# Gate and up projections as 2x2 block products with seven products, in a two-block transformer kernel

## The reference

```python
# first block, D_FF = 2816
h = rmsnorm(x, norm_ffn)
x = x + (silu(h @ w_gate) * (h @ w_up)) @ w_down
...
# second block, D_FF_2 = 4096
h = _rmsnorm(x, mlp_norm_w)
x = x + square(relu(h @ w_up)) @ w_down
```

## Time and profile before

| what | value |
|---|---|
| median of 3 runs | 3381.11 us (3380.43 to 3384.27) |
| the profiled execution | 3385.8 us, its span 3384.0 us |
| TensorE busy | 3128.2 us, 92% |
| VectorE, ScalarE, GpSimd busy | 36%, 31%, 30% |
| moved by DMA | 177.27 MB, 52 GB/s on average |

### The profile page before, as it was taken

How to read it: one execution, slowest core, us unless ns; L and a number is a source line. 1 busy time by engine, 2 the same in 40 slices (tenths; PEclk the granted TensorE clock), 3 DMA queues, 4 the chain that set the end, 5 groups by cost and what they waited for, 6 DMA issues and landing times.

```text
span 3384.0 us, 36901 instructions
## 1 busy us (share of the span) xinstructions
PE 3128.2 (92%) x14350; PEld 2388.2 (71%) x14350; DVE 1232.6 (36%) x2192; ACT 1065.8 (31%) x1490; POOL 1015.0 (30%) x424
## 2 busy tenths in 40 slices
PE   5989888888989999999999898896999999999998
PEld 3556556566678788888887665564777788888887
DVE  4347777766132111111113555554553211112122
ACT  3235554444433211111113344443553211111110
POOL 4322233221234343243246200013102332323241
PEclk8879999899999999999999999997999999999999
DMA  5311112111152111111111311001002111111112
GB/s 158 98 31 32 38 32 57 38 39 49 51 168 84 48 48 51 44 50 50 44 48 43 107 30 31 14 24 31 19 4 81 44 54 46 50 43 56 44 50 68
DMA packets 261934, 177.27 MB, mean 52 GB/s; under 512 B 20724, under 2 KB 248948, under 8 KB 261236
## 3 DMA queue, kind: packets, MB, share of 16 engines
q1 hardware_dynamic: 261816, 175.69, 18.0%
HBM read 142.60 MB, written 25.20 MB: 50 GB/s over the span
## 4 chain that ended last, share of the span: by engine, by line
PE 79%; DVE 8%; ACT 5%; issue 5%; POOL 2%; DMA 1%; SPq 0%; ACTq 0%; DVEq 0%; POOLq 0%
PE big L832 64%; PE big L990 4%; PE tbank L1013 3%; PE obank L1031 3%; PE big L964 2%; PE obank L1028 2%; PE big L861 1%; DVE tally_a L1665 1%; DVE dprob L1729 1%; POOL w_lo L1909 1%; DVE prob L1729 1%; ACT prob L1218 1%; DVE g_lo L1775 0%; DMA x_res<-x_spill 0%; ACT mpt L1176 0%
## 5 line engine op out<-in xcount | busy, mean ns | idle before, releaser
L832 PE MATMUL big<-g_hi,w_hi 128*128 128x512 f32 x3328 | 1074.4, 404 | 61.5 <-ACT gst_b L1250 21.1
L832 PE MATMUL big<-g_lo,w_hi 128*128 128x512 f32 x3328 | 1040.6, 394 | 0.0
L832 PE MATMUL big<-g_hi,w_lo 128*128 128x512 f32 x3328 | 1037.1, 393 | 0.0
L832 PEld LDWEIGHTS big<-g_hi,w_hi 128*128 128x128 f32 x3328 | 609.0, 191 | 265.7 <-issue 142.9
L832 PEld LDWEIGHTS big<-g_lo,w_hi 128*128 128x128 f32 x3328 | 633.0, 190 | 137.0 <-issue 0.7
L832 PEld LDWEIGHTS big<-g_hi,w_lo 128*128 128x128 f32 x3328 | 631.5, 190 | 137.4 <-issue 0.4
L1909 POOL TENSOR_TENSOR w_lo<-w_raw,w_hi 128x1024 fp32r<-128x1024 f32 x99 | 241.4, 2439 | 593.0 <-ACT w_hi L1152 593.0
L1998 POOL TENSOR_TENSOR w_lo<-w_raw,w_hi 128x1024 fp32r<-128x1024 f32 x76 | 181.9, 2393 | 64.2 <-ACT w_hi L1371 64.2
L1840 DVE TENSOR_TENSOR x_res<-big,x_res 128x1024 f32 x40 | 49.0, 1225 | 382.1 <-PE big L832 382.1
L2024 POOL TENSOR_TENSOR w_lo<-w_raw,w_hi 128x1024 fp32r<-128x1024 f32 x40 | 95.7, 2393 | 273.2 <-ACT w_hi L1399 273.2
L1176 ACT ACTIVATE pt<-tbank 128x512 f32<-128x512 f32 (+1 forms) x160 | 88.2, 555 | 221.3 <-PE tbank L1013 221.3
(11 more groups left out here) (268 smaller groups left out, 3498.0 us busy)
## 6 DMA issues: line engine op xcount, KB each, us to landing
w_raw<-in_w_up SPq DMA_DIRECT2D x54, 512.0 KB, 3.9
w_raw<-in_w_in SPq DMA_DIRECT2D x51, 512.0 KB, 4.2
w_raw<-in_w_down SPq DMA_DIRECT2D x48, 512.0 KB, 3.9
w_raw<-in_w_gate SPq DMA_DIRECT2D x22, 512.0 KB, 3.8
rot<-rope_in SPq DMA_DIRECT2D x68, 128.0 KB, 2.3
g_spill<-gst_b SPq DMA_DIRECT2D x16, 512.0 KB, 3.0
x_res<-x_spill SPq DMA_DIRECT2D x2, 4096.0 KB, 14.0
w_raw<-in_w_out SPq DMA_DIRECT2D x16, 512.0 KB, 4.3
```

The lines of the kernel that those rows point to most:

```text
L832: ins = pe.matmul(out[0:m, HALF * h:HALF * h + HALF], w[slot][:, col:col + m], x[:, HALF * h:HALF * h + HALF], start=(n == 0 and q == 0), ...
```

## The change

Both feed-forward blocks are changed in how the up side is computed. A job takes two column tiles together: gate and up tile of the same features in `mlp1` (22 jobs), two neighbouring up tiles in `mlp2` (16 jobs). The job is a 2x2 block product: the weights are A (tile 1 or 2, chunks 0 to 3 or 4 to 7), the activations B (chunks 0 to 3 or 4 to 7, tokens 0 to 511 or 512 to 1023). It is done by seven block products in place of eight, of sums and differences of blocks:

- Weight operands per job: A11, A12 and A22 as they are, and the sums S1 = A21 + A22, S2 = S1 - A11, S4 = S2 - A12, S3 = A21 - A11, in 128x512 each. GpSimd makes the four sums and all seven low parts, ScalarE the seven high parts. The order of use is A11, S1, A12, S4, S2, A22, S3. Each operand has one place, which is free again when the job before has done that product. Both raw tiles are loaded together, once the S3 low part of the job before is done.
- Activation operands, once per block: B11, B21, B22 and T1 to T4, each 4 chunks of 128x512 in a high and a low part. VectorE makes them during `out` and right behind it, in place of `g2h` and `g2l`; T4 and T3 and their low parts, and that of T2, come last.
- A product is 4 x 3 matmuls of 128x512 into a PSUM bank of its own: `tbank` (2), `obank` (2) and three halves of `big`. ScalarE copies out the first two, and VectorE adds the others in seven steps into two rows (`crow`, two buffers), which are the tile pair. VectorE scales both rows by `r_rep` and forms the activation: SiLU between by ScalarE in `mlp1`, a square of the positive part for each row in `mlp2`.
- The activations go to DRAM (`a_spill`, 512 KB per tile) and come back ahead of the down side, in groups of (8, 4, 4, 6) tiles in `mlp1` and 4 of 8 in `mlp2`. ScalarE makes the high part of a reloaded tile, VectorE the low part (`act_lo`). All up jobs come first, then all down groups. The down products stay as they were, 6 matmuls per chunk.
- The first matmul of the sum of squares now stands behind the first product of the first job. The last group of `mlp1` keeps its norm work.

```diff
+    B11, T1, B21, B22, T2, T4, T3 = range(7)
+    A11, S1, A12, S4, S2, A22, S3 = range(7)
...
+    READ_AT = {2: 1, 4: 2, 3: 3, 6: 5, 5: 7}
...
+    BLOCKED = ["mlp1", "mlp2"]
+    groups1 = [(0, 8), (8, 4), (12, 4), (16, 6)] if "mlp1" in BLOCKED else [(0, 8), (8, 8), (16, 6)]
...
+    def down_buffers(stage, gi):
+        return (g1h, g1l) if gi % 2 == (1 if stage in BLOCKED else 0) else (g2h, g2l)
...
+    def slot_free(stage, q, n):
+        if n:
+            return s_st.sem, s_st.base(stage) + 7 * (n - 1) + q + 1
+        w = last_outs(stage)
+        return s_big.at("w", w[0]) if q < 2 else (s_big.at("w", w[1]) if q < 4 else s_big.at("ss", "ffn" if stage == "mlp1" else "mlp2"))
...
+                banks = [tbank[0][:, :], tbank[1][:, :], obank[0][:, :], obank[1][:, :], big[p0][:, 0:HALF], big[p0][:, HALF:T], big[1 - p0][:, 0:HALF]]
+                def block_product(q, at_job):
+                    pe.wait_ge(s_al.sem, at_job(7, al0 + q + 1))
+                    for k in range(4):
+                        for z, (w, x) in enumerate(((ah, bh), (ah, bl), (al, bh))):
+                            ins = pe.matmul(banks[q], w[q][:, P * k:P * k + P], x[q][:, k, :], start=(k == 0 and z == 0),
+                                            stop=(k == 3 and z == 2))
+                    ins.then_inc(s_st.sem, 1)
...
+                with pe.Fori(1, NJ, 1) as i:
+                    for q in range(7):
+                        if q < 2:
+                            pe.wait_ge(s_ar.sem, i * 2 + (ar0 + q - 1))
+                        else:
+                            pe.wait_ge(s_dr.sem, i * 7 + (dr0 - 7 + READ_AT[q]))
+                        block_product(q, lambda m, c: i * m + c)
...
+                            if gi == 0:
+                                pe.wait_ge(s_dr.sem, dr0 + 7 * NJ)
+                                pe.wait_ge(s_ar.sem, ar0 + 2 * NJ)
+                            ready = (lambda k: s_xlo.at(stage, f0 + k)) if u == 0 else (lambda k: None)
...
+        def weight_hi(stage, q, n):
+            ah, _, az = a_ops[last_outs(stage)[1] % 2]
+            src = block_source(q, *w_raw)
+            if q in (A11, A12, A22):
+                for t in range(2):
+                    act.wait_ge(*s_ur[t].at(stage, n))
+            else:
+                act.wait_ge(*s_as.at(stage, q, n))
+            act.wait_ge(*slot_free(stage, q, n))
+            act.activation(ah[q][:, :], az[q][:, :] if src is None else src, ACT.Copy).then_inc(*s_ah.mark(stage, q, n))
...
+                for m in range(NJ):
+                    c = crow[m % 2]
+                    ahead = m + 1 < NJ
...
+                    read(m, 0, c[1][:, 0:HALF])
+                    read(m, 1, c[1][:, HALF:T], -1.0)
+                    if m == 0:
+                        act.wait_ge(*s_bf.at(out_stage, T4))
...
+                        weight_hi(stage, S3, 0)
+                    if ahead:
+                        for q in (A11, S1, A12):
+                            weight_hi(stage, q, m + 1)
...
+                    if ahead:
+                        for q in (S4, S2):
+                            weight_hi(stage, q, m + 1)
...
+                    if ahead:
+                        weight_hi(stage, A22, m + 1)
+                    if one:
+                        act.wait_ge(*s_fn.at(stage, m, 0))
+                        act.activation(c[0][:, :], c[0][:, :], ACT.Silu).then_inc(*s_si.mark(stage, m))
+                    if ahead:
+                        weight_hi(stage, S3, m + 1)
...
+                def add(m, what, dest, one_, other, *waits, op=ALU.add):
+                    for w in waits:
+                        dve.wait_ge(*w)
+                    if isinstance(other, int):
+                        dve.wait_ge(s_st.sem, st0 + 7 * m + other + 1)
+                    dve.tensor_tensor(dest, one_, banks[other] if isinstance(other, int) else other, op).then_inc(*s_dr.mark(stage, m, what))
+                def act_lo(gi, k):
+                    gh, gl = down_buffers(stage, gi)
...
+                def form(m, r):
+                    c = crow[m % 2]
+                    dve.wait_ge(*s_fn.at(stage, m, 2 * r))
+                    if one:
+                        dve.wait_ge(*s_si.at(stage, m))
+                        ins = dve.tensor_tensor(c[1][:, :], c[1][:, :], c[0][:, :], ALU.mult)
+                    else:
+                        ins = dve.scalar_tensor_tensor(out=c[r][:, :], in0=c[r][:, :], scalar=0.0, in1=c[r][:, :], op0=ALU.max, op1=ALU.mult)
...
+                block_lo(T2)
+                for m in range(NJ):
+                    c, final = crow[m % 2], m == NJ - 1
+                    c11, c12, c21, c22 = c[0][:, 0:HALF], c[0][:, HALF:T], c[1][:, 0:HALF], c[1][:, HALF:T]
+                    at_ = lambda what: s_dr.at(stage, m, what)
+                    add(m, "c11", c11, c21, 2, s_ar.at(stage, m, 0), *([s_asp[m % 2].at(stage, m - 2)] if m >= 2 else []))
+                    if m == 0:
+                        block_lo(T4)
+                        block_lo(T3)
+                    if final:
+                        for k in range(2):
+                            act_lo(0, k)
+                    add(m, "u2", c21, c21, 4, at_("c11"))
+                    add(m, "p3", c12, c21, 3, at_("u2"), op=ALU.subtract)
+                    add(m, "c12", c12, c12, c22, at_("p3"), s_ar.at(stage, m, 1))
+                    scale_row(m, 0, at_("c12"))
+                    if not one:
+                        form(m, 0)
+                    if final:
+                        for k in range(2, 4):
+                            act_lo(0, k)
+                    add(m, "u3", c21, c21, 6, at_("p3"))
+                    add(m, "c22", c22, c22, c21, at_("u3"))
+                    add(m, "c21", c21, c21, 5, at_("c22"))
+                    if final:
+                        for k in range(4, 6):
+                            act_lo(0, k)
+                    scale_row(m, 1, at_("c21"))
+                    form(m, 1)
...
+        def weight_sum(stage, n, q, a, b, op, *waits):
+            for w in waits:
+                pool.wait_ge(*w)
+            dest = s2t if q == S2 else a_ops[last_outs(stage)[1] % 2][2][q]
+            pool.tensor_tensor(dest[:, :], a, b, op).then_inc(*s_as.mark(stage, q, n))
+        def weight_lo(stage, n, q):
+            ah, al, az = a_ops[last_outs(stage)[1] % 2]
+            src = block_source(q, *w_raw)
+            pool.wait_ge(*s_ah.at(stage, q, n))
...
+            pool.tensor_tensor(al[q][:, :], az[q][:, :] if src is None else src, ah[q][:, :].bitcast(F32),
+                               ALU.subtract).then_inc(*s_al.mark(stage, n, q))
+        def weight_lo_early(stage, n):
+            az = a_ops[last_outs(stage)[1] % 2][2]
+            weight_sum(stage, n, S1, w_raw[1][:, 0:HALF], w_raw[1][:, HALF:T], ALU.add,
+                       s_ur[0].at(stage, n), s_ur[1].at(stage, n), slot_free(stage, S1, n))
+            weight_sum(stage, n, S2, az[S1][:, :], w_raw[0][:, 0:HALF], ALU.subtract, s_as.at(stage, S1, n),
+                       *([s_al.at(stage, n - 1, S2)] if n else []))
+            weight_lo(stage, n, A11)
+            weight_lo(stage, n, S1)
+        def weight_lo_middle(stage, n):
+            weight_sum(stage, n, S4, s2t[:, :], w_raw[0][:, HALF:T], ALU.subtract, slot_free(stage, S4, n))
+            weight_lo(stage, n, A12)
+            weight_lo(stage, n, S4)
+        def weight_lo_late(stage, n):
+            weight_lo(stage, n, S2)
+            weight_lo(stage, n, A22)
+            weight_sum(stage, n, S3, w_raw[1][:, 0:HALF], w_raw[0][:, 0:HALF], ALU.subtract, slot_free(stage, S3, n))
+            weight_lo(stage, n, S3)
...
+                def up_weights(n):
+                    if n:
+                        sp.wait_ge(*s_al.at(stage, n - 1, S3))
+                    else:
+                        sp.wait_ge(s_wlo.sem, last_outs(stage)[1] + 1)
+                    for t in range(2):
+                        w, f = ((a["w_gate"][0], a["w_up"][0])[t], n) if one else (a["w_up_2"][0], 2 * n + t)
+                        sp.dma_start(raw(t, DC, P), cols(w, P * f)).then_inc(*s_ur[t].mark(stage, n, by=16))
+                def spill(n):
+                    sp.wait_ge(*s_fn.at(stage, n, 3))
+                    if one:
+                        sp.dma_start(a_spill[n], crow[n % 2][1][:, :]).then_inc(*s_asp[n % 2].mark(stage, n, by=16))
+                    else:
...
+                def reload(gi, k):
+                    f = groups[gi][0] + k
+                    sp.wait_ge(*s_asp[(f if one else f // 2) % 2].at(stage, f if one else f // 2))
+                    sp.dma_start(down_buffers(stage, gi)[1][:, k, :].bitcast(F32), a_spill[f]).then_inc(*s_rl[k].mark(stage, f, by=16))
+                up_weights(0)
+                for n in range(1, NJ):
+                    up_weights(n)
+                    if n >= 2:
+                        spill(n - 2)
+                sp.wait_ge(*s_al.at(stage, NJ - 1, S3))
```

(64 more changed lines are left out.)

249 lines of the change are left out of this document (248 added, 1 removed).

## The result

The changed kernel takes 3494.92 us (median of 4 runs, 3493.19 to 3500.05); the kernel before, timed beside it on the same chip, takes 3382.69 (3380.43 to 3385.92). The ratio is 1.0334 (95% interval 1.0316 to 1.0351): 3.3% slower. The forecast was 3450 us, with a range of 3350 to 3500 and 0.78 on slower. The profiled execution took 3500.05 us, 114.3 more than the profiled one of before (3385.8).

What follows compares the result with a forecast made beforehand. TensorE bounds the kernel now; after the change GpSimd's ring of load and instructions would. 41 + 6 + 22 = 69 us more gives 3454.8 us profiled, 3450 us median; forecast's own range 3420 to 3475, wide range 3350 to 3500.

Steps and rivals of the forecast that it cites:

- the ring: Up-side jobs: weight load, 11 GpSimd instructions, load again; 20.3 us undisturbed, 22.85 with collisions and small waits, against 21.77 now.
- the pair of loads: A job's two raw weight loads, issue to landing: 5.5 us, bounds 5.1 and 6.3.
- S3's exposure: ScalarE's rounding of S3, summed just before it is needed, with two hand-overs: 0.7 us a job.
- Rival (1): Seventh product's VectorE work does not collide, or GpSimd loses nothing: ring 20.3 us, 3354 us in all; chance 0.15.
- (3): GpSimd's instruction at its lower bound of 1.20 us, load 5.2: ring 21.7 us, 3406 us in all; chance 0.13.
- (4): The ring stays under TensorE's 19.05 us and the change gives what it says: 3294 us in all; chance 0.05.
- Rival (2): The 512-column GpSimd instruction takes 1.35 us, or the load 6.3: ring 23.7 us, 3481 us in all; chance 0.17.
- The collisions: VectorE work with both inputs in SBUF holds GpSimd up: 2.5 us a job, bounds 0 and 3.
- the first half: VectorE's c12 and first scaling, in GpSimd's load gap: no cost, but 1.5 us (2.5 in `mlp2`) if outside it.
- The sum: Both blocks: 41 us for jobs, 6 for first jobs, 22 from up to down, 69 us more in all.
- the first jobs: Start of each block: job 1's first product goes at 30 us against 27.9 now; 3 us each, 6 in all.
- pauses: From up to down, TensorE idle before the first down product: 10 us in `mlp1`, 12 in `mlp2`, 22 in all.

## Why the prediction was right, and where its terms were off

**The bound and its change: right.** The pace passes from TensorE to the ring of load and GpSimd. The ring without disturbance was forecast at 20.3 us and measured at 20.49 and 20.70 (VectorE's part cut away). The 512-column instruction takes 1.29 us with starts 1.25 apart (forecast 1.27), the pair of loads 5.8 us (5.5), S3's exposure 0.74 (0.7). The figure of 1.34 us that I estimated from the Trainium skill (GPSIMD Engine Reference, section Elementwise — side-by-side cycle accounting) was too high; the trace has 1.29. Rival (1) had no collision, (3) a whole ring of 21.7 us and (4) one under 19.05; none held. Rival (2) named 3481 us by an instruction of 1.35 us or a load of 6.3; the time came nearer to it than to the forecast, but neither was so, and it came there for other reasons.

**The collisions: right in kind, too small in number.** Forecast 2.5 us a job, measured 3.0 and 3.4 by the run with VectorE's part cut away, 3.0 and 3.6 by the count in the trace. Each meeting cost what it should. The step that failed is "the first half comes after the fifth product, in the gap in which GpSimd waits for its load: no cost". I had priced its falling out of the gap (1.5 and 2.5 us) and then charged none of it; it falls out in about every second job, and costs there just those 1.5 and 2.5 us. I charged 22.85 us for all jobs; they took 23.44 and 24.07.

**The sum counted some of it twice.** Made anew from the same terms, for the stretch from job to job: the first jobs 30 against 27.9 us, 2.1 each and not 3, 4.2 in all; 34 periods with 1.08 more, 36.7; the last job of a block, which ends for TensorE at 19.05, 2.7 less than 21.77, -5.4; pauses 22. That is 57.5, not 69. In the forecast the last job's 3.8 us stand in the period and again in the pause, which is counted from 19.05, and the first jobs are charged both with the ring and with their own excess. The two blocks became 112 us longer, so the terms missed 55 us, not 43:

- jobs: 20 x (23.44 - 21.77) + 14 x (24.07 - 21.77) = 66 us against 37: 29 us;
- first jobs: 36.0 and 36.4 against 30: 12 us;
- pauses: 28.5 idle and 4.8 by TensorE's slower clock behind them, 33 against 22: 11 us;
- last jobs: 19.4 and 21.0 us where I had 19.05: 2 us.

With these the sum gives 112 us, as measured; nothing is left over for the down products.

**The first jobs: failed.** I had 12.5 us for VectorE's work ahead of its three low parts of 2048 columns, 2.3 us for each of them, and no collision. The work ahead took 14.2 us (1132.9 to 1147.05). In the trace (VectorE, then GpSimd, `mlp1`):

```profile
1147.05 3.19 DVE L2102 TENSOR_TENSOR b_lo<-b_raw,b_hi 128x2048 fp32r<-128x2048 f32 x1
1150.76 6.04 DVE L2102 TENSOR_TENSOR b_lo<-b_raw,b_hi 128x2048 fp32r<-128x2048 f32 x2
...
1146.81 1.28 POOL L2312 TENSOR_TENSOR a_lo<-s_raw,a_hi 128x512 fp32r<-128x512 f32 x1 [6.41 <-ACT a_hi L1308]
1148.06 3.32 POOL L2312 TENSOR_TENSOR a_lo<-w_raw,a_hi 128x512 fp32r<-128x512 f32 x1
1151.34 3.32 POOL L2304 TENSOR_TENSOR a_raw<-w_raw,w_raw 128x512 f32<-128x512 f32 x1
```

A GpSimd instruction of 1.29 us takes 3.32 beside one of 2048 columns. Before that, GpSimd stands for 6.4 us until ScalarE has rounded S2, which stands in ScalarE's queue behind the rounding of T4 (1144.30 to 1146.2). The load of job 1 went out 25 us after the start, not 19. This is read from the trace; no run tested it by itself.

**The pause: right in its cause, too short.** The spill and the reloads behind it went as forecast. Tile 3 landed 25.2 us after the start of the last job (forecast 25). But I had VectorE make low part 3 right behind tile 3's rounding, at 27.3. In its queue low parts 0 and 1 wait for their reloads ahead of u2, and u2, p3, c12 and the scaling, some 4 us, come behind them and only then low parts 2 and 3: low part 3 is done after 31.3 us and c21 after 33.4, not 29.4. In `mlp2` the pause is 14.4 us against 12. To this comes TensorE's clock, which the forecast left out. In the changed kernel, around the pause and around one idle stretch of 4.95 us between jobs (columns as above):

```profile
1480.00:1497.50 17.50, 12.92 (x58) 10.36 (x56) 8.59 (x10) 3.38 (x6) 10.74 (x7) 1.00 0.30 90
1497.50:1501.00 3.50, 3.13 (x8) 2.51 (x9) 0.00 (x0) 0.69 (x2) 3.50 (x4) 0.51 0.00 0
...
1671.20:1675.00 3.80, 3.80 (x9) 3.02 (x10) 3.77 (x4) 0.00 (x0) 0.00 (x0) 0.50 0.01 2
1675.00:1690.00 15.00, 15.00 (x67) 12.40 (x67) 6.86 (x6) 3.07 (x3) 2.51 (x1) 1.00 0.61 185
```

The granted clock is at half, its level of 1.2 GHz, when TensorE starts again. What that costs is read from TensorE's own rows: the second down product of `mlp1` starts where the first, begun at 1671.16, ends.

```profile
1683.49 0.62 PE L893 MATMUL big<-g_hi,w_lo 128*128 128x512 f32 x2
1683.95 0.61 PE L893 MATMUL big<-g_hi,w_hi 128*128 128x512 f32 x2
```

The first down product takes 12.8 us, and by the same reading 13.75 in `mlp2` (3123.24 to 3136.99), instead of 10.9: 1.9 and 2.9 us more, which nothing hides.

**The forecast of 3450 was 45 us low**: the terms missed 55 us, 2 us came behind `mlp2`, where the result is written out, and the double counting gave some 12 back. The direction and the bound were argued and came true. The number was not as good: the time lies 20 us above the forecast's own 3420 to 3475, and the wide range, 3350 to 3500, held it by 5 us only, with an upper end that was set by rival (2), whose causes did not occur. That is luck.

## What to carry to other kernels

When matmuls are traded for elementwise work, draw the ring of the weakest engine with its loads in it and compare its period with TensorE's, not the engines' shares of the span. GpSimd pays for each VectorE instruction with two SBUF inputs that meets it with nearly its whole length (1.0 of 1.23 us). Here it paid to move work from the engine that sets the ring to the one that collides with it, and to release buffers as soon as their last reader is through. A queue in order must not have an instruction that waits for a DMA ahead of those that free PSUM.
